# Band attention scores over all 128 partition rows: one head's queries with zeros beside them, against the keys of both heads

## The chip, the cores and the metric

The kernel runs on one core of a Trainium2 chip. The metric is the device time of one execution in microseconds (us), taken as the median of several runs.

## What is computed

One inference step of two encoder layers over 544 tokens: a prompt of 512 and a sample of 32 that also has cached keys and values. Each layer is a SwiGLU feed-forward block, a mixer and another feed-forward block, with norms around each. The mixer of the even layer is two attentions side by side, A (latent attention, "mla") and B (band attention). Only B is touched:

```python
def band_attend(q, k, v, q_pos, k_pos, rel_table):
    b, nq, h, d = q.shape                       # 8 heads, d = 64
    rel = jnp.clip(q_pos[:, None] - k_pos[None, :], -B_MAX_REL, B_MAX_REL) + B_MAX_REL
    bias = rel_table.astype(jnp.float32)[:, rel]
    s = jnp.einsum('bqhd,bkhd->bhqk', q, k).astype(jnp.float32) * HEAD_SCALE + bias[None]
    p = attn_probs(s, (k_pos >= 0)[None, :])
    return jnp.einsum('bhqk,bkhd->bqhd', p.astype(v.dtype), v).reshape(b, nq, h * d)
```

The prompt's queries see their own chunk of 64 and the eight before it, which for 512 tokens is every earlier chunk. The 32 sample queries see 256 cached keys and their own 32.

## The kernel before

Everything lies transposed in SBUF: channels on the 128 partitions, tokens along the free axis. Weights come from HBM through `w_raw`; ScalarE writes their high part `w_hi` (L351) and VectorE the low part `w_lo` (L358), and TensorE forms each product of the large projections from three matmuls (L417 to L419). Six sub-layers run one after the other: ffn, even, ffn, ffn, odd, ffn.

In the even sub-layer, `qkvb` `[128, 12, 544]` holds the queries (tiles 0 to 3), keys (4 to 7) and values (8 to 11) of the band attention. A tile of 128 rows holds two heads: the even head in rows 0 to 63, the odd one in rows 64 to 127. Then come, in TensorE's order: the latent attention (`attention("mla")`), a short preparation (`band_ready`, L753 to L785), the band attention (`attention("band")`), and the output projection.

Each attention works through items. The first 32 are the prompt's: 8 heads, each with 4 blocks of 128 queries against 128, 256, 384 and 512 keys. The last two are the sample's, four heads each, every head in 32 output rows of its own. For each item TensorE forms the scores in one of three PSUM banks (L570 for band, L564 for mla, L580 for the odd layer's "swa"), adds masks or the relative bias by a matmul with the identity (L549: `rel_hi` and `rel_lo` for band, one mask of 128 columns for mla), VectorE takes the row maximum (L1255), ScalarE the exponentials (L889), TensorE turns the probabilities (L615), ScalarE copies them back (L900), TensorE multiplies them with the values (L639, for the sample L653), and VectorE scales the result (L1279, L1282). The loop of TensorE runs the scores of item n, then the turn of item n - 3 and the values of item n - 4, so that other work of TensorE lies between an item's scores and its turn. After every second head, four blocks of outputs are turned (L666). Scores of the sample are L586 and L549 (bias), then for each head L597 (its own 32 keys) and L600 (256 cached keys, `kB_cache`).

The scores of one band head use only its own 64 rows of both operands. Those of mla use 96 rows (64 channels and 32 rotary ones).

`band_ready` turns the values of `qkvb` into `vB` (L765), forms the bias tiles (L768, L772, L775), and waits for ScalarE and VectorE to have copied them out (L1124, L1427, L1430) and for two DMAs, which GpSimd issues once the last mla scores are done (L1507 to L1509). GpSimd then waits for the fourth sub-layer (L1511). `qtA` and `ktA`, the operands of the mla scores, lie from `kt_at` up to `kt_at + 43008`; nothing reads them after the last mla scores.

Of the kernel before, what the change touches and what calls it, by code (L numbers as in the profile page):

```python
# [25 lines left out]
F32 = mybir.dt.float32  # L26
# [5 lines left out]
P = 128  # L32
D = 1024
KD = D // P
SEQ, DEC, PAST = 512, 32, 256
T = SEQ + DEC
# [9 lines left out]
NOPE, ROPE, HD = 64, 32, 64  # L46
# [5 lines left out]
SK = DEC + PAST  # L52
# [83 lines left out]
def build(nc, ins, outs):  # L136
    with ExitStack() as ctx:
        cursor = [(nc.sbuf_base + 31) // 32 * 32]

        def place(name, shape, dt, at=None):  # L140

            size = 4 * int(np.prod(shape[1:]))
            offset = cursor[0] if at is None else at
            if at is None:
                cursor[0] += (size + 31) // 32 * 32
            return nc.alloc_sbuf_tensor_at(name, shape, dt, offset=offset)
# [37 lines left out]
        qkvb = place("qkvb", [P, 12, T], F32, at=arena)  # L184
        kt_at = arena + 26112
# [21 lines left out]
        kB_cache = place("kB_cache", [P, 4, PAST], F32, at=kt_at + 14336)  # L207
        rel_hi = place("rel_hi", [P, NH, 2 * P], F32R, at=kt_at + 18432)
        relS_hi = place("relS_hi", [P, 2, SK], F32R, at=kt_at + 26624)
        rel_lo = place("rel_lo", [P, NH, 2 * P], F32R, at=va_at)  # L210
        relS_lo = place("relS_lo", [P, 2, SK], F32R, at=va_at + 8192)

# [26 lines left out]
        psum = ctx.enter_context(nc.psum_tensor("psum", [P, 8, 512], F32))  # L239

        def sem(name):
            return ctx.enter_context(nc.semaphore(name))
# [41 lines left out]
        kpe_spread = sem("kpe_spread")  # L284
        band_in = sem("band_in")
        band_prep = sem("band_prep")
        rel_in = sem("rel_in")
        rel_shifted = sem("rel_shifted")
        mask_in = sem("mask_in")
# [132 lines left out]
        def _(pe):  # L422
# [93 lines left out]
            def out_projection(s):  # L516
# [7 lines left out]
                for m, H in out_order(SUBS[s]):  # L524
# [10 lines left out]
                    out_half(s, g + m // 2, (g + m // 2) % 2, m % 2, H, m == 0, mid)  # L535
                    before = (m, H)

            def attention(name, between=None):

                items, done = ATT[name]  # L540
# [10 lines left out]
                def scores(n):  # L551

                    it, bank = items[n], n % 3
                    if name == "swa" and n in (8, 16):

                        pe.wait_ge(c_roped, n + 2)
                    if n >= 3:

                        pe.wait_ge(exp_done, base + n - 2)
                    if it["kind"] == "prompt":  # L560
                        i, w = it["i"], it["width"]
                        q = slice(P * i, P * (i + 1))
                        if name == "mla":
                            nc.tensor.matmul(psum[:, bank, 0:w], qtA[:, it["h"], q], ktA[:, it["h"], 0:w],  # L564
                                             start=True, stop=True)
                            mm = add(psum[:, bank, w - P:w], maskE[:, P:2 * P])
                        elif name == "band":
                            h, near = it["h"], min(w, 2 * P)
                            r = slice(64 * (h % 2), 64 * (h % 2) + 64)
                            nc.tensor.matmul(psum[:, bank, 0:w], qkvb[r, h // 2, q], qkvb[r, 4 + h // 2, 0:w],  # L570
                                             start=True, stop=True)

                            add(psum[:, bank, w - near:w], rel_hi[:, h, 2 * P - near:2 * P])
                            mm = add(psum[:, bank, w - near:w], rel_lo[:, h, 2 * P - near:2 * P])
                        else:
                            lo = P * max(i - 1, 0)
                            for d in range(2):
                                h = it["h"] + 2 * d
                                r = slice(64 * (h % 2), 64 * (h % 2) + 64)
                                nc.tensor.matmul(psum[:, bank, d * w:(d + 1) * w], qtC[r, h // 2, q],  # L580
                                                 kdup[r, h // 8, lo:lo + w], start=True, stop=True)
                                mm = add(psum[:, bank, d * w:(d + 1) * w], maskC[:, 2 * P - w:2 * P])
                    else:
                        if name == "band":

                            nc.tensor.matmul(psum[:, bank, 0:SK], unit[:], relS_hi[:, it["h"] // 4, :],  # L586
                                             start=True, stop=True)
                            add(psum[:, bank, 0:SK], relS_lo[:, it["h"] // 4, :])
                        for d in range(4):
                            h = it["h"] + d  # L590
                            rows = slice(32 * d, 32 * d + 32)
                            r = slice(64 * (h % 2), 64 * (h % 2) + 64)
                            if name == "mla":
                                mm = nc.tensor.matmul(psum[rows, bank, 0:SK], qtA[:, h, SEQ:T],
                                                      ktA[:, h, SEQ:KEYS_A], start=True, stop=True)
                            elif name == "band":
                                nc.tensor.matmul(psum[rows, bank, 0:DEC], qkvb[r, h // 2, SEQ:T],  # L597
                                                 qkvb[r, 4 + h // 2, SEQ:T], start=False, stop=True,
                                                 skip_group_check=True)
                                mm = nc.tensor.matmul(psum[rows, bank, DEC:SK], qkvb[r, h // 2, SEQ:T],  # L600
                                                      kB_cache[r, h // 2, :], start=False, stop=True,
                                                      skip_group_check=True)
                            else:
                                mm = nc.tensor.matmul(psum[rows, bank, 0:DEC + P], qtC[r, h // 2, SEQ:T],
                                                      kdup[r, h // 8, SEQ:KEYS_C], start=True, stop=True)
                    mm.then_inc(s_ready, 1)
# [146 lines left out]
            def band_ready(s):  # L753

                def job(j):
                    if j == 5:
                        pe.wait_ge(rel_shifted, 10)
                        pe.wait_ge(o_lo, O0["band"])
                    if j >= 8:

                        pe.wait_ge(band_act if j % 2 == 0 else band_dve, (j - 8) // 2 + 1)
                    if j < 5:
                        n = P if j < 4 else DEC
                        for v in range(4):
                            mm = nc.tensor.transpose(psum[0:n, j, v * P:(v + 1) * P],  # L765
                                                     qkvb[:, 8 + v, j * P:j * P + n], ident[:])
                    elif j < 9:
                        nc.tensor.matmul(psum[:, j % 8, :], flips[:, 0, :],  # L768
                                         hankel[:, 2 * (j - 5):2 * (j - 4), :].rearrange("p h k -> p (h k)"),
                                         start=True, stop=True)  # L770
                        for h in range(2):
                            mm = nc.tensor.matmul(psum[:, j % 8, 2 * P * h:2 * P * (h + 1)], identE[:], maskE[:],  # L772
                                                  start=False, stop=True, skip_group_check=True)
                    else:
                        mm = nc.tensor.matmul(psum[:, j % 8, 0:SK], flips[:, 1, :], hankelS[:, j - 9, :],  # L775
                                              start=True, stop=True)
                    mm.then_inc(band_prep, 1)

                pe.wait_ge(exp_done, A0["band"])
                pe.wait_ge(pt_ready, A0["band"])  # L780
                for j in range(11):
                    job(j)
                pe.wait_ge(band_act, 9)
                pe.wait_ge(band_dve, 8)
                pe.wait_ge(band_in, 16 * 2)  # L785

            pe.wait_ge(consts_in, 16 * 3)
            for s, kind in enumerate(SUBS):
# [9 lines left out]
                elif kind == "even":  # L798
                    for f in range(2, 8):
# [3 lines left out]
                        if f == 4:  # L803

                            pe.wait_ge(proj_read, P0[s] + 4)
                            for H in range(2):
                                pe.wait_ge(lat_sq, 3 * H + 3)
                                for t in range(2):
                                    nc.tensor.matmul(psum[:, 4 + H, 0:TH], ones[:], scratch[:, 2 * H + t, :],
                                                     start=t == 0, stop=t == 1)  # L810
                                nc.tensor.matmul(psum[:, 6 + H, 0:TH], ones[:], lat_rstd[:, 1, HALF[H]],
                                                 start=True, stop=True).then_inc(lat_stat, 1)
# [655 lines left out]
        def _(pool):  # L1468
# [4 lines left out]
            rows = slice(NOPE, QK)  # L1473
# [33 lines left out]
            pool.wait_ge(s_ready, A0["band"])  # L1507
            load(vB_cache[:], ins["band_v_cache"]).then_inc(band_in, 16)
            load(kB_cache[:], ins["band_k_cache"]).then_inc(band_in, 16)  # L1509
            s = 4  # L1510
            pool.wait_ge(y_ready, 16 * s)  # L1511
            load(ropeC[:], ins["rope_swa"]).then_inc(odd_in, 16)
# [127 lines left out]
```

## Time and profile before

| | |
|---|---|
| median of 3 runs | 2331.65 us (2329.54 to 2334.93) |
| span of the profiled execution (first to last instruction) | 2321.0 us |
| what lies around that span, against the median | 10.65 us |
| TensorE busy | 2276.4 us, 98% |
| TensorE weight loads busy | 2172.6 us, 94% |
| VectorE busy | 1033.6 us, 45% |
| ScalarE busy | 777.3 us, 33% |
| GpSimd busy | 20.4 us, 1% |
| mean granted clock of TensorE | 0.973 of 2.4 GHz |
| HBM | 75 GB/s over the span |

The profile gives no time for the profiled execution other than its span, so a time for a kernel is read here as span plus 10.65 us. Busy time of TensorE is modelled at the ends of its instructions: a record lasts longer than its turn in the pipeline, so the cost of a matmul is read from the distance between the starts of two records. An fp32 matmul shows as two records. A granted clock of 1.00 is 2.4 GHz, and 0.50 is 1.2 GHz.

### The profile page before, as it was taken

How to read it: one execution, taken by the hardware profiler on the slowest of the kernel's cores; microseconds unless marked ns; L12 is line 12 of the kernel's file. 1: busy time of each engine (PE TensorE's matmuls, PEld its weight loads, DVE VectorE, ACT ScalarE, POOL GpSimd, SP SyncE). 2: the span in 40 equal slices, each digit the busy share in tenths (PEclk: the TensorE clock that was granted, in tenths of full speed). 3: DMA queues.
4: the chain of work that ended last, by engine and by line, in shares of the span. 5: the costliest groups of instructions: out<-in, count | busy, mean ns of one | idle time of the engine just before them, and what ended most of it. 6: DMA issues, size and time to landing. Idle time of an engine off the chain costs nothing.

```text
span 2321.0 us, 41718 instructions
## 1 busy us (share of the span) xinstructions
PE 2276.4 (98%) x16934; PEld 2172.6 (94%) x16934; DVE 1033.6 (45%) x1992; ACT 777.3 (33%) x1566; POOL 20.4 (1%) x42
## 2 busy tenths in 40 slices
PE   7999999999999999999999999999999999999997
PEld 6999999998767999999999999999987799999997
DVE  4544412656532274444126544512666555444313
ACT  4332322423532353333124323322425453332211
POOL 0000000001000000000000000000000000000000
PEclk9999999999955999999999999999999999999999
DMA  3222322124000122222221222322220022222221
GB/s 114 92 90 90 104 76 93 59 82 144 19 1 1 55 67 97 88 81 98 76 93 55 91 90 90 96 83 93 71 85 1 19 73 86 79 89 90 99 76 63
DMA packets 48489, 176.94 MB, mean 76 GB/s; under 512 B 5808, under 2 KB 10240, under 8 KB 48144
## 3 DMA queue, kind: packets, MB, share of 16 engines
q1 hardware_dynamic: 46144, 166.66, 22.0%
q0 software_dynamic: 2256, 9.03, 1.2%
q8 instruction: 63, 1.03, 0.2%
q14 instruction: 26, 0.21, 0.0%
HBM read 168.93 MB, written 5.36 MB: 75 GB/s over the span
## 4 chain that ended last, share of the span: by engine, by line
PE 94%; DVE 3%; ACT 2%; issue 0%; DMA 0%; SPq 0%; DVEq 0%; ACTq 0%
PE psum L418 26%; PE psum L417 26%; PE psum L419 26%; PE psum L639 3%; PE psum L494 2%; PE psum L549 2%; PE psum L570 2%; PE psum L446 2%; PE psum L615 2%; PE psum L580 2%; PE psum L564 1%; PE psum L653 1%; DVE w_lo L358 1%; ACT xhi L964 0%; DVE rstd L1165 0%; DVE y_ffn L1173 0%
## 5 line engine op out<-in xcount | busy, mean ns | idle before, releaser
L417 PE MATMUL psum<-xhi,w_hi 128*128 128x272 f32 x3488 | 1031.7, 296 | 19.5 <-DVE w_lo L358 16.8
L418 PE MATMUL psum<-xlo,w_hi 128*128 128x272 f32 x3488 | 1005.5, 288 | 0.0
L419 PE MATMUL psum<-xhi,w_lo 128*128 128x272 f32 x3488 | 1003.4, 288 | 0.0
L417 PEld LDWEIGHTS psum<-xhi,w_hi 128*128 128x128 f32 x3488 | 657.9, 189 | 25.0 <-issue 16.8
L418 PEld LDWEIGHTS psum<-xlo,w_hi 128*128 128x128 f32 x3488 | 657.5, 188 | 5.3
L419 PEld LDWEIGHTS psum<-xhi,w_lo 128*128 128x128 f32 x3488 | 656.3, 188 | 0.0
L358 DVE TENSOR_TENSOR w_lo<-w_raw,w_hi 128x1024 fp32r<-128x1024 f32 (+1 forms) x286 | 363.0, 1308 | 444.3 <-ACT w_hi L351 443.9
L417 PE MATMUL psum<-h_hi,w_hi 128*128 128x272 f32 x1408 | 417.2, 296 | 0.0
L418 PE MATMUL psum<-h_lo,w_hi 128*128 128x272 f32 x1408 | 405.7, 288 | 0.0
L419 PE MATMUL psum<-h_hi,w_lo 128*128 128x272 f32 x1408 | 403.9, 287 | 0.0
L351 ACT ACTIVATE w_hi<-w_raw 128x1024 fp32r<-128x1024 f32 (+1 forms) x286 | 307.4, 1120 | 80.5 <-PE psum L419 70.2
L417 PEld LDWEIGHTS psum<-h_hi,w_hi 128*128 128x128 f32 x1408 | 265.1, 188 | 2.4
L418 PEld LDWEIGHTS psum<-h_lo,w_hi 128*128 128x128 f32 x1408 | 264.9, 188 | 2.4
L419 PEld LDWEIGHTS psum<-h_hi,w_lo 128*128 128x128 f32 x1408 | 264.4, 188 | 0.0
L1007 ACT ACTIVATE scratch<-scratch 128x272 f32<-128x272 f32 x160 | 69.0, 431 | 551.3 <-DVE scratch L1222 551.3
L1222 DVE TENSOR_TENSOR scratch<-psum,rstd 128x272 f32<-128x272 f32 x176 | 77.7, 441 | 313.1 <-PE psum L419 311.4
L1022 ACT ACTIVATE y_ffn<-psum 128x272 f32<-128x272 f32 (+1 forms) x64 | 25.3, 396 | 379.6 <-PE psum L419 379.6
L1231 DVE TENSOR_TENSOR h_lo<-scratch,h_hi 128x272 f32 (+1 forms) x176 | 77.8, 442 | 119.3 <-ACT h_hi L1009 111.4
L1255 DVE TENSOR_REDUCE soft<-psum 128x1 f32<-128x128 f32 (+5 forms) x104 | 54.3, 523 | 118.0 <-PE psum L549 113.4
L1165 DVE RECIPROCAL rstd<-rstd 128x272 f32<-128x272 f32 x24 | 44.4, 1851 | 140.0 <-ACT rstd L947 106.9
L1009 ACT ACTIVATE h_hi<-scratch 128x272 f32 (+1 forms) x160 | 69.1, 432 | 95.7 <-DVE scratch L1228 95.7
L1228 DVE TENSOR_TENSOR scratch<-scratch 128x272 f32<-128x272 f32 x176 | 77.8, 442 | 26.7 <-ACT scratch L1007 8.2
(219 smaller groups left out, 1696.4 us busy)
## 6 DMA issues: line engine op xcount, KB each, us to landing
w_raw<-in_w_gate_up SPq DMA_DIRECT2D x176, 512.0 KB, 4.0
w_raw<-in_w_down SPq DMA_DIRECT2D x64, 704.0 KB, 5.0
w_raw<-in_even_in SPq DMA_DIRECT2D x16, 512.0 KB, 3.5
w_raw<-in_odd_in SPq DMA_DIRECT2D x10, 512.0 KB, 3.7
w_raw<-in_even_out SPq DMA_DIRECT2D x8, 512.0 KB, 4.1
w_raw<-in_odd_out SPq DMA_DIRECT2D x8, 512.0 KB, 3.8
x<-in_x SPq DMA_DIRECT2D x2, 1088.0 KB, 7.5
out_band_kv<-qkvb POOLq DMA_DIRECT2D x1, 2176.0 KB, 9.0
```

Source lines behind the costliest of these rows:

```text
L351: nc.scalar.activation(w_hi[:, 2 * par + u, 0:n], w_raw[:, u, 0:n], ACT.Copy).then_inc(w_hi_done, 1)
L358: nc.vector.tensor_tensor(w_lo[:, 2 * par + u, 0:n], w_raw[:, u, 0:n], w_hi[:, 2 * par + u, 0:n].bitcast(F32), ALU.subtract).then_inc(w_lo ...
L417: nc.tensor.matmul(out, s_hi, m_hi, start=first, stop=False)
L418: nc.tensor.matmul(out, s_hi, m_lo, start=False, stop=False)
L419: return nc.tensor.matmul(out, s_lo, m_hi, start=False, stop=last)
L639: mm = nc.tensor.matmul(psum[:, bank, HD * d:HD * (d + 1)], probsT[:, n % 2, p:p + P], v, start=j == 0, stop=j == per - 1)
L1007: nc.scalar.activation(scratch[:, 2 * H, :], scratch[:, 2 * H, :], ACT.Silu).then_inc(silu_done, 1)
L1009: nc.scalar.activation(h_hi[:, f, HALF[H]], scratch[:, 2 * H, :], ACT.Copy).then_inc(hhi_ready, 1)
L1222: nc.vector.tensor_tensor(scratch[:, 2 * H, :], psum[:, bank, 0:TH], rstd[:, HALF[H]], ALU.mult).then_inc(gate_scaled, 1)
L1228: nc.vector.tensor_tensor(scratch[:, 2 * H, :], scratch[:, 2 * H, :], scratch[:, 2 * H + 1, :], ALU.mult).then_inc(h_ready, 1)
L1231: nc.vector.tensor_tensor(h_lo[:, f, HALF[H]], scratch[:, 2 * H, :], h_hi[:, f, HALF[H]].bitcast(F32), ALU.subtract).then_inc(hlo_ready, 1)
L1255: red = nc.vector.tensor_reduce(part[:, 0:heads], scores, AX_X, ALU.max, negate=True)
```

## The change

A new tile `qB_odd` `[128, 4, 544]` takes the odd heads' queries: GpSimd copies them into its rows 64 to 127, sets its rows 0 to 63 to zero, and then sets rows 64 to 127 of the query tiles of `qkvb` to zero. So `qkvb` holds each even head's queries with zeros beside them, and `qB_odd` each odd head's. The score matmuls take all 128 rows of both operands; the other head's keys meet zeros. `qB_odd` lies at `kt_at + 31232`, within what was `qtA`. The rest of the kernel stays as it was.

```diff
+        qB_odd = place("qB_odd", [P, 4, T], F32, at=kt_at + 31232)
...
+            def q_alone(h):
+
+                return qB_odd if h % 2 else qkvb
...
                             h, near = it["h"], min(w, 2 * P)
-                            r = slice(64 * (h % 2), 64 * (h % 2) + 64)
-                            nc.tensor.matmul(psum[:, bank, 0:w], qkvb[r, h // 2, q], qkvb[r, 4 + h // 2, 0:w],
+                            nc.tensor.matmul(psum[:, bank, 0:w], q_alone(h)[:, h // 2, q], qkvb[:, 4 + h // 2, 0:w],
                                              start=True, stop=True)
...
-                                nc.tensor.matmul(psum[rows, bank, 0:DEC], qkvb[r, h // 2, SEQ:T],
-                                                 qkvb[r, 4 + h // 2, SEQ:T], start=False, stop=True,
+                                nc.tensor.matmul(psum[rows, bank, 0:DEC], q_alone(h)[:, h // 2, SEQ:T],
+                                                 qkvb[:, 4 + h // 2, SEQ:T], start=False, stop=True,
                                                  skip_group_check=True)
-                                mm = nc.tensor.matmul(psum[rows, bank, DEC:SK], qkvb[r, h // 2, SEQ:T],
-                                                      kB_cache[r, h // 2, :], start=False, stop=True,
+                                mm = nc.tensor.matmul(psum[rows, bank, DEC:SK], q_alone(h)[:, h // 2, SEQ:T],
+                                                      kB_cache[:, h // 2, :], start=False, stop=True,
                                                       skip_group_check=True)
...
                 pe.wait_ge(band_act, 9)
                 pe.wait_ge(band_dve, 8)
+                pe.wait_ge(q_parted, 3)
                 pe.wait_ge(band_in, 16 * 2)
...
             load(vB_cache[:], ins["band_v_cache"]).then_inc(band_in, 16)
             load(kB_cache[:], ins["band_k_cache"]).then_inc(band_in, 16)
+            nc.gpsimd.tensor_copy(qB_odd[HD:P, :, :], qkvb[HD:P, 0:4, :]).then_inc(q_parted, 1)
+            nc.gpsimd.memset(qB_odd[0:HD, :, :], 0.0).then_inc(q_parted, 1)
+            pool.wait_ge(q_parted, 1)
+            nc.gpsimd.memset(qkvb[HD:P, 0:4, :], 0.0).then_inc(q_parted, 1)
             s = 4
```

## Rows read from the trace of the kernel before

**Rows 1.** The page: TensorE's clock in 40 slices, and the chain by engine.

```profile
PEclk9999999999955999999999999999999999999999
...
PE 94%; DVE 3%; ACT 2%; issue 0%; DMA 0%; SPq 0%; DVEq 0%; ACTq 0%
```

**Rows 2.** Windows: mla, band, swa items (span, PE, PEld, DVE, ACT, POOL, PEclk, DMA).

```profile
576.60:622.70 46.10, 45.26 (x319) 38.05 (x319) 25.90 (x87) 30.11 (x94) 0.00 (x0) 1.00 0.01 1
...
646.20:754.70 108.50, 108.46 (x352) 77.14 (x352) 27.33 (x89) 31.45 (x96) 0.00 (x0) 0.51 0.00 1
...
1724.90:1819.50 94.60, 94.24 (x529) 68.24 (x528) 63.24 (x236) 49.88 (x190) 0.00 (x0) 1.00 0.00 1
```

**Rows 3.** Timeline, TensorE: band items of 128 and 512 keys (start us, us).

```profile
739.77 0.79 PE L570 MATMUL psum<-qkvb 64*128 64x128 f32 x2
...
740.98 0.65 PE L615 MATMUL psum<-ident,probsE 128*128 128x128 f32 x2
...
750.32 2.07 PE L570 MATMUL psum<-qkvb 64*128 64x512 f32 x2
...
752.91 0.41 PE L615 MATMUL psum<-ident,probsE 128*128 128x128 f32 x1
```

**Rows 4.** Timeline, TensorE: mla items of 512 and 128 keys, at full clock.

```profile
583.60 1.08 PE L564 MATMUL psum<-ktA,qtA 96*128 96x512 f32 x2
...
584.58 0.27 PE L615 MATMUL psum<-ident,probsE 128*128 128x128 f32 x1
...
585.52 0.44 PE L564 MATMUL psum<-ktA,qtA 96*128 96x128 f32 x2
...
585.86 0.41 PE L615 MATMUL psum<-ident,probsE 128*128 128x128 f32 x2
```

**Rows 5.** Timeline, TensorE: swa scores of 128 and 256 keys, 64 rows, full clock.

```profile
1725.58 0.48 PE L580 MATMUL psum<-kdup,qtC 64*128 64x128 f32 x2
...
1726.25 0.70 PE L580 MATMUL psum<-kdup,qtC 64*128 64x256 f32 x2
...
1727.19 0.70 PE L580 MATMUL psum<-kdup,qtC 64*128 64x256 f32 x2
```

**Rows 6.** Windows, TensorE: where its clock moves (span, PE busy, PEclk, DMA).

```profile
633.40:634.90 1.50, 0.02 (x1) 1.00 0.00 0
...
635.00:635.50 0.50, 0.50 (x4) 0.58 0.00 0
...
638.50:639.00 0.50, 0.50 (x6) 1.00 0.00 0
...
648.50:649.00 0.50, 0.50 (x3) 0.73 0.00 0
...
757.50:758.00 0.50, 0.50 (x3) 0.54 0.00 0
```

**Rows 7.** Timeline: the second bias add at full clock, near the start of band.

```profile
647.62 0.39 PE L549 MATMUL psum<-rel_hi,identE 128*128 128x256 f32 x1
647.85 0.28 PE L549 MATMUL psum<-rel_lo,identE 128*128 128x256 f32 x1
```

**Rows 8.** Timeline: the start of the first and of the second sample item of band.

```profile
754.68 0.59 PE L586 MATMUL psum<-relS_hi,identE 128*128 128x288 f32 x1
...
757.34 0.59 PE L586 MATMUL psum<-relS_hi,identE 128*128 128x288 f32 x1
```

**Rows 9.** Timeline: GpSimd's last DMA issue, and what the first band scores wait for.

```profile
625.71 0.55 POOL L1509 DMA_DIRECT2D kB_cache<-in_band_k_cache  x1
...
646.24 0.46 PE L570 MATMUL psum<-qkvb 64*128 64x128 f32 x2 [1.22 <-ACT relS_hi L1124]
```

**Rows 10.** Groups by line: GpSimd's memsets, and VectorE's slowest elementwise rows (busy us, mean ns).

```profile
L1479 POOL MEMSET ckv_hi<- 128x96 f32 x1 | 0.2, 217 | 0.0
...
L1627 POOL MEMSET const-float32-0.0<- 128x1 f32 x1 | 0.1, 93 | 0.3 <-issue 0.3
...
L1165 DVE RECIPROCAL rstd<-rstd 128x272 f32<-128x272 f32 x24 | 44.4, 1851 | 140.0 <-ACT rstd L947 106.9 <-ACT rstd L953 33.2
```

More of the change, by code:

```diff
@@ L286, in build @@
         band_prep = sem("band_prep")
+        q_parted = sem("q_parted")
         rel_in = sem("rel_in")
```

## Prediction

> **What bounds the kernel now.** I read the page first. The chain that ended last is TensorE for 94% of the span, so a change is worth what it takes from TensorE's own time or from a wait of TensorE. The slices of the clock show one place, slices 12 and 13, where the granted clock is 5 tenths instead of 9 or more [rows 1]. One slice is 58 us, so something like 110 us run at 1.2 GHz. The windows by stage put it in the band attention: its 32 prompt items fill 646.2 to 754.7 us with TensorE busy for 108.46 of 108.50 us and a mean clock of 0.51, while the mla attention, which has the same number of items with the same numbers of keys, takes 46.1 us at 1.00 [rows 2]. VectorE is busy for 27.3 us and ScalarE for 31.5 us of the band stretch [rows 2], so neither is the bound there; what sets the pace is TensorE.
>
> I then took the stage apart by the timeline. From the start of an item's scores to the turn that follows them, a band item takes 1.21 us for 128 keys (739.77 to 740.98) and 2.59 us for 512 (750.32 to 752.91) [rows 3]. The same distance for mla is 0.34 us (585.52 to 585.86) and 0.98 us (583.60 to 584.58) [rows 4]. In mla each further 128 keys cost (0.98 - 0.34) / 3 = 0.213 us, which is 4 x 128 columns at 2.4 GHz: an fp32 score goes over its columns four times, an added mask once. What is left of 0.34 after 0.213 for the scores and 0.053 for the mask is 0.07 us that doesn't depend on width. For the swa scores, which use 64 rows at full clock, the distance from one score to the next is 0.67 us for 128 keys and 0.94 us for 256 [rows 5]; the step of 0.27 us is again four passes and one added mask, but 0.67 - 0.267 leaves 0.40 us fixed. So scores of 64 rows cost 0.40 - 0.07 = 0.33 us an item beside others of 128 rows, at full clock, whatever their width. For band at 1.2 GHz, 1.21 us less 0.427 (scores) and 0.213 (two bias adds) leaves 0.57 us, and 2.59 less 1.707 and 0.427 leaves 0.46 us.
>
> The Trainium skill, TensorEngine Tiling (Array Packing), Key Properties, says that changing the tiling mode, not just the tile, drains TensorE. The trace agrees, with that 0.33 us.
>
> Last I looked where the clock moves [rows 6]. It falls within 635.0 to 635.5 us, after the mla sample values and a stretch in which TensorE was busy for 0.02 of 1.50 us, and is back at 638.5, while TensorE turned the values of band (L765), all over 128 rows. It falls again within 648.5 to 649.0, after a wait of 1.22 us ahead of the first band scores [rows 9] and two and a half items of 64-row scores, and then stays at 1.2 GHz until 757.5 to 758.0 without an idle moment, that is until the last 64-row score of 512 keys is 5 us past. Scores of 64 rows alone don't pull it down: the swa stage runs 94.6 us at 1.00 with them [rows 2]. But after a fall, no stretch made up largely of them brought it back, and a stretch of full-row work did.
>
> **The change part by part.** (1) *The 32 prompt items.* The new items are mla items with more bias. To mla's 46.1 us [rows 2] comes first a bias add of 256 columns instead of 128 in 24 of 32 items: 24 x 128 / 2.4 GHz = 1.3 us. Then a second bias add in all 32: at least its columns, 256 / 2.4 GHz = 0.107 us, at most the 0.23 us from `rel_hi` to `rel_lo` [rows 7]. mla's fixed 0.07 us for a score and an add makes 0.035 us each, so I take 0.107 + 0.035 = 0.14 us, times 32 = 4.5 us (3.4 to 7.4). Together 51.9 us (50.8 to 54.8) for what took 108.4 us (646.24 [rows 9] to 754.68 [rows 8]): **56.5 us** less. Some 10.6 us of this, 32 x 0.33, are the switches between 64 and 128 rows, and 46 us the clock. VectorE's 27.3 and ScalarE's 31.5 us stay below 51.9, and mla ran with 25.9 and 30.1 in 46.1 us [rows 2], so they should not become the bound.
>
> (2) *The sample items.* The first one, 754.68 to 757.34, ran at 1.2 GHz [rows 8], as did the first 0.6 us of the second. At full clock 2.66 us become 1.33 and 0.6 become 0.3: **1.6 us** less (1.0 to 1.7, since some of it is not streaming). That their scores take 128 rows by 32 instead of 64 by 32 I cost at nothing: four heads lie in four column groups either way. All that follows, the sample values and the output projection, was at full clock and stays.
>
> (3) *GpSimd's copy and two memsets*, each of 64 rows x 2176 columns. GpSimd's DMA issue ends at 625.71 + 0.55 = 626.3 us, and the scores could start at 646.24 [rows 9], so 19.9 us cover them. A memset takes (217 - 93) / 95 = 1.3 ns a column [rows 10]: 2.9 us each, 5.8 for two. A GpSimd copy is not in the trace. From below it costs the memset's 2.9 us; from above I take VectorE's slowest elementwise row, 1851 ns for 272 columns or 6.8 ns a column [rows 10], which makes 14.8 us. I take 4 us, near the memset, since a copy has the same output and one input. Sum 9.8 us, done at about 636 us (8.7 to 20.6 us, 635.0 to 646.9). So the cost is **nothing**, 0.7 us at the upper end. Without the cover the wait on `q_parted` would hold every band score, and with it all that follows on TensorE. Behind the three instructions GpSimd has nothing to do before the fourth sub-layer, and no DMA issue of it or of SP is moved past them. VectorE works on the bias rows in the same stretch; should its 2.2 us of `hankel` shifts (L1416), which lie on the chain, take twice as long beside GpSimd, that would be 2.2 us. I take 0 and keep 2.2 for the range.
>
> (4) *The clock's fall at 648.5.* The 1.22 us wait ahead of the first score stays, since it is for the last bias rows of ScalarE and VectorE [rows 9]. If the clock falls there all the same and comes back as at 638.5, after 3.4 us, it costs half of that, 1.7 us. The sample values may bring such a fall in one place more or fewer than before. I take 0 for both and keep -1.7 and +3.4.
>
> Sum: 56.5 + 1.6 = 58.1 us off. The span goes from 2321.0 to 2262.9 us and, with the 10.65 us around it, the median from 2331.65 to **2273.5 us**. The bounds: at best 57.6 + 1.7 + 1.7 = 61 us off, at worst 53.6 + 1.0 - 0.7 - 2.2 - 3.4 = 48.3. The median itself moves by up to 3 us among the runs shown. The forecast's own range is 2268 to 2284.
>
> **The rivals.** *The clock stays at 1.2 GHz.* Half of each score's rows are zeros, and what the clock follows may not be the rows that an instruction names. For it: TensorE was already busy throughout at 0.51 [rows 2], so it isn't plain that another form of the same scores wakes it. Against it: the fall is gone after full-row work at 638.5, and mla with 96 rows never lost the clock. Then only the switches go, 32 x 0.33 = 10.6 us, or 32 x (0.46 - 0.14) = 10.2 to 32 x (0.57 - 0.14) = 13.8 from the items at 1.2 GHz: **2321 us** (2317 to 2322).
>
> The Trainium skill, TensorE: Matmul & The Clock Gate, Part 1, says that the clock follows how busy TensorE has been of late and that sustained work releases it. By that rule the band stretch should have been at full speed already, and more rows would change nothing in it: the rival's time. The trace doesn't agree, with 0.51 at 108.46 of 108.50 us busy; I leave the rival its chance for that.
>
> *The clock comes back only for parts of the stage.* The turns and the values of 64 columns lie between the scores, and falls and returns could alternate. For it: two falls within 14 us before [rows 6]. Against it: mla holds 1.00 through the same alternation. With the stage at half clock for half of its work it takes 1.5 x 51.9 = 78 us, and the time is **2300 us**, anything from 2285 to 2315.
>
> *GpSimd is late, and the kernel slower.* Place: the wait on `q_parted` at the end of `band_ready`. GpSimd needs more than 19.9 us before it costs anything and 19.9 + 58.1 = 78 us before it decides: 12 ns a column over 3 x 2176 columns. At 14 ns a column it takes 91 us, and the time is 2273.5 + 71.5 = **2345 us**. Against it: its memset row has 1.3 ns a column, and the slowest elementwise row of any engine 6.8 [rows 10].
>
> **How the numbers follow.** Forecast 0.82, clock stays low 0.08, partly low 0.06, GpSimd late 0.02, and 0.02 for a stage whose time doesn't move for reasons that I don't see. A difference under 0.2%, 4.7 us, is about what a measurement of this kernel can't tell from none. The first three are faster by more than that, save for a little of the second: faster 0.95, same 0.03, slower 0.02. For 8 in 10, the range takes the forecast's own, 2 us more below, and the edge of the partly low case: 2266 to 2287.
>
> **What would show it.** In the profile after, slices 12 and 13 should have no 5. From the first L570 to the first L586 it should be 50 to 55 us at a mean clock of 0.97 or more; a band item from score to turn about 0.45 us for 128 keys and 1.15 for 512. GpSimd's three instructions should end by about 636 us and not release L570. The prediction is wrong if the clock stays at 0.5 in spite of full rows (the stage then near 98 us), if the first L570 waits for GpSimd, or if the waits of TensorE for L889 or L1282 grow once it runs twice as fast.

## The result and the profile after

The changed kernel takes 2265.68 us (median of 4 runs, 2263.59 to 2268.53) against 2330.61 for the kernel before: a ratio of 0.9725, with a 95% interval of 0.971 to 0.9739. That is 64.9 us less. The forecast was 2273.5 us, in a range of 2266 to 2287, so the time lies 7.8 us under the point and 0.3 us under the lower end of the range, which is less than the spread of its own runs. In the profiled executions the span went from 2321.0 to 2266.7 us, 54.3 us less; why this is 10.6 us short of the difference of the medians is taken up below.

The page of the kernel after shows the clock by slices without the two fives, and TensorE's share of the chain as it was:

```profile
span 2266.7 us, 41722 instructions
...
PEclk9999999999999999999999999999999999999999
...
PE 94%; DVE 3%; ACT 2%; issue 0%; DMA 0%; SPq 0%; DVEq 0%; ACTq 0%
```

Windows of the kernel after, by stage: the mla items, the band items, the band sample items with their values, the swa items. The columns are those of [rows 2].

```profile
576.60:622.70 46.10, 44.44 (x313) 37.08 (x311) 26.32 (x87) 29.38 (x93) 0.00 (x0) 1.00 0.01 1
649.10:699.20 50.10, 49.80 (x351) 42.92 (x351) 25.89 (x87) 30.23 (x94) 0.00 (x0) 1.00 0.01 1
699.20:710.00 10.80, 10.80 (x123) 7.93 (x122) 4.50 (x19) 4.17 (x13) 0.00 (x0) 1.00 0.01 2
1668.10:1762.70 94.60, 94.23 (x529) 68.22 (x528) 63.24 (x236) 49.97 (x190) 0.00 (x0) 1.00 0.00 1
```

The 32 band items take 50.1 us at 1.00 where they took 108.5 at 0.51, with as many matmul records (351 and 352; some are missing from any profile) and about the same work on VectorE and ScalarE (25.9 and 30.2 us busy, 27.3 and 31.5 before). The swa stage, which nobody touched, takes its 94.6 us again.

Timeline of TensorE in the kernel after, an item of 512 keys and one of 128; L575 is what was L570, and L620 what was L615:

```profile
656.82 1.08 PE L575 MATMUL psum<-qkvb,qB_odd 128*128 128x512 f32 x2
657.34 0.68 PE L555 MATMUL psum<-rel_hi,identE 128*128 128x256 f32 x1
657.86 0.28 PE L555 MATMUL psum<-rel_lo,identE 128*128 128x256 f32 x1
657.98 0.27 PE L620 MATMUL psum<-ident,probsE 128*128 128x128 f32 x1
...
658.93 0.44 PE L575 MATMUL psum<-qkvb 128*128 128x128 f32 x2
...
659.38 0.41 PE L620 MATMUL psum<-ident,probsE 128*128 128x128 f32 x2
```

From score to turn an item now takes 1.16 us (657.98 - 656.82) instead of 2.59 and 0.45 us instead of 1.21 [rows 3]. The second bias add costs 0.12 us, its columns and almost nothing else (657.98 - 657.86).

Timeline of the kernel after, GpSimd and what the first scores wait for:

```profile
627.01 0.55 POOL L1515 DMA_DIRECT2D kB_cache<-in_band_k_cache  x1
...
627.61 2.00 POOL L1516 COPY qB_odd<-qkvb 64x2176 f32<-64x2176 f32 x1
...
629.66 1.90 POOL L1517 MEMSET qB_odd<- 64x2176 f32 x1
...
631.62 1.91 POOL L1519 MEMSET qkvb<- 64x2176 f32 x1
...
637.85 2.19 DVE L1422 TENSOR_SCALAR hankel<-hankel,rel_far 128x256 f32<-128x256 f32 x8
...
649.14 0.46 PE L575 MATMUL psum<-qkvb 128*128 128x128 f32 x2 [1.22 <-ACT relS_hi L1130]
```

GpSimd's three instructions, which part the queries, end at 633.5 us. The first score waits as before, for the bias rows and for the same 1.22 us [rows 9].

Windows of TensorE in the kernel after, where its clock is low (columns as in [rows 6]):

```profile
641.50:644.00 2.50, 2.50 (x6) 0.50 0.00 0
...
1774.50:1784.50 10.00, 10.00 (x53) 0.50 0.01 2
```

Two low stretches of the kernel before have moved: the one at 635 us begins at 641 and now lies on the bias matmuls, and one follows the swa stage, with its sample values and the start of the output projection, for 10 us instead of 3.4. A third, of 3.4 us, stands at 518 us, where before had none.

The stretch at 1774.5 us is a second place where TensorE is busy without a break (10.00 of 10.00 us above, and its last idle moment 3.6 us earlier was 0.28 us long) and yet loses the clock. Most of it are the values of the sample, 64 columns each, on 128 rows by 32 columns of the array and on 32 by 32 in turn:

```profile
1770.86 0.27 PE L658 MATMUL psum<-vC_cache,probsTC 128*32 128x64 f32 x2 [0.28 <-DVE osbC L1288]
...
1778.54 0.42 PE L658 MATMUL psum<-vC_cache,probsTC 128*32 128x64 f32 x2
1778.89 0.42 PE L658 MATMUL psum<-vC,probsTC 32*32 32x64 f32 x2
```

### The profile page after: what moved, and what is told of

Same layout as the page of the kernel before. It is cut to its first block, busy times and chain, and to the rows that moved or that the text cites. A ratio compares the mean times of both kernels' runs of the same rounds, so it can differ in the third digit from the quotient of the medians.

```text
span 2266.7 us, 41722 instructions
## 1 busy us (share of the span) xinstructions
PE 2220.2 (98%) x16934; PEld 2139.1 (94%) x16934; DVE 1033.2 (46%) x1992; ACT 777.1 (34%) x1566; POOL 26.3 (1%) x45
## 4 chain that ended last, share of the span: by engine, by line
PE 94%; DVE 3%; ACT 2%; issue 0%; DMA 0%; SPq 0%; DVEq 0%; ACTq 0%
PE psum L420 27%; PE psum L419 26%; PE psum L421 26%; PE psum L644 2%; PE psum L496 2%; PE psum L448 2%; PE psum L585 2%; PE psum L620 1%; PE psum L555 1%; PE psum L575 1%; PE psum L658 1%; PE psum L570 1%; DVE w_lo L360 1%; ACT xhi L970 0%; DVE rstd L1171 0%; DVE y_ffn L1179 0%
## 5 line engine op out<-in xcount | busy, mean ns | idle before, releaser
L1261 DVE TENSOR_REDUCE soft<-psum 128x1 f32<-128x128 f32 (+5 forms) x104 | 54.2, 522 | 60.1 <-PE psum L555 58.2
```

What stands on the lines that cost most here:

```text
L1261: red = nc.vector.tensor_reduce(part[:, 0:heads], scores, AX_X, ALU.max, negate=True)
```

## The experiments

All medians are of four or more runs unless said otherwise. The ratios are to the kernel before, measured beside each run: 2327.04 us for again, warm64, nozero and half, 2331.74 for late and swa_full, 2329.56 for pause and late3, 2330.61 for the changed kernel itself. So a difference between medians of two lines of this list is uncertain by some microseconds. Here "stage" is the time from the first band score to the first sample item, which the change takes from 108.4 to 50.1 us.

**again.** The kernel before, unchanged.

> The kernel before, unchanged, profiled once more, because its first profile has a span of 2321.0 us while its runs have a median of 2330.6. My reading: the prompt part of the band stage lasts 108.4 us at half clock in every execution, and what differs is short falls of the clock elsewhere, some 8 us in all against the first profile. The rival is that the band stage itself was shorter in the profiled execution than in most: then the first L570 to the first L586 would take about 116 us here. Time 2330 (2326 to 2335).

2327.72 us against 2327.04 for before, a ratio of 1.0005 (0.9988 to 1.0023). Windows of its band stage:

```profile
646.50:754.60 108.10, 108.10 (x351) 76.84 (x351) 27.36 (x89) 31.46 (x96) 0.00 (x0) 0.51 0.00 1
```

The stage is as long as in the first profile, but this profile too fell on a short execution, with a span of 2319.8 us. Time less span is about 1.8 us in every run (2.0 to 2.2 in late), so the 10.65 us of the front table are not a fixed surrounding: about 8 of them are a difference between executions. Half of the other 22 runs have a span near 2325.1 us and a mean clock of 0.971, seven more a span near 2327.8; the profiled one has 0.974 and 2319.8. Lost to the low clock are 2325.1 x 0.029 = 67.4 and 2319.8 x 0.026 = 60.3 us: 7 us, which covers the difference of 5.3 (a last digit of the clock is 2.3 us of span). So the longer executions have more low clock, but no profile shows where. One run of 22 took 2310.96 us at a clock of 0.979. It is 10.6 us shorter than the profiled one, which has only 3.4 us of low clock ahead of the stage and some 8 at the very end (half of them, 6 us, is all that they can give back), so the long fall itself was probably shorter in that run; no profile shows this either.

**warm64.** The kernel before with the pause ahead of the scores filled:

```diff
                 for j in range(11):
                     job(j)
+                pe.wait_ge(band_dve, 2)
+                for _i in range(2):
+                    nc.tensor.matmul(psum[:, 3, :], flips[:, 0, :],
+                                     hankel[:, 0:2, :].rearrange("p h k -> p (h k)"), start=True, stop=True)
```

> The kernel before with two more matmuls of 128 rows x 512 columns, written to a bank that nobody reads, in the pause of 1.22 us ahead of the first band scores; the scores stay at 64 rows. Theory A (64-row scores keep a clock that they find, as in the swa stage, and only can't bring it back): no fall at the start, the stage takes the 50.1 us of the changed kernel plus 32 x 0.33 = 10.6, about 61 us, and the time is 2330.6 - 47 = 2283 us. Theory B (a stage of 64-row scores falls whatever goes before it): the stage stays near 108 us, at 0.50, and the time is 2331 us, the same as before within 2 us.

2282.46 us, a ratio of 0.9796 (0.9774 to 0.9818). Timeline and then windows of its band stage:

```profile
647.75 1.88 PE L785 MATMUL psum<-hankel,flips 128*128 128x512 f32 x4
649.56 0.48 PE L570 MATMUL psum<-qkvb 64*128 64x128 f32 x2
```

```profile
649.60:709.70 60.10, 60.10 (x352) 43.44 (x352) 26.56 (x87) 30.63 (x94) 0.00 (x0) 1.00 0.00 1
```

Theory A holds, to within a microsecond. With 64-row scores all through, the stage ran at 1.00 once the pause ahead of it was gone, and the times of all four runs say the same. With the pause and full-row scores behind it, in the changed kernel, it ran at 1.00 too. So the fall at 648.5 [rows 6] took both, the pause and the 64-row scores. This run also parts the gain in two: 108.4 - 60.1 = 48.3 us are the clock, and 60.1 - 50.1 = 10.0 us what 64-row scores cost at the same clock, 0.31 us an item, which is put down here to the switching between 64 and 128 rows.

**nozero.** The changed kernel without GpSimd's part, both heads' queries in the same rows:

```diff
             def q_alone(h):
-                return qB_odd if h % 2 else qkvb
+                return qkvb
...
-                pe.wait_ge(q_parted, 3)
...
-            nc.gpsimd.tensor_copy(qB_odd[HD:P, :, :], qkvb[HD:P, 0:4, :]).then_inc(q_parted, 1)
-            nc.gpsimd.memset(qB_odd[0:HD, :, :], 0.0).then_inc(q_parted, 1)
-            pool.wait_ge(q_parted, 1)
-            nc.gpsimd.memset(qkvb[HD:P, 0:4, :], 0.0).then_inc(q_parted, 1)
```

> The changed kernel without the parting: GpSimd copies and clears nothing, and the scores of both heads of a pair take all 128 rows of the same queries, so each score is the sum of two heads' scores. This tells whether zeros in half of the rows matter to the clock or to the time. If only the rows that the instruction names count: 2266 us, as the changed kernel, the stage 50 us at 1.00. If zeros weigh less: some stretches of the changed kernel that ran at 0.5 (about 3.4 us at 640 us) are gone and the time is 2 to 4 us lower. If GpSimd's 5.8 us of work cost anything, that goes too: up to 2 us.

2265.89 us (2265.79 to 2266.08), a ratio of 0.9728 (0.9712 to 0.9744), against 2265.68 for the changed kernel; its stage lasts from 646.6 to 696.7 us:

```profile
646.60:696.70 50.10, 49.84 (x352) 42.93 (x352) 25.99 (x87) 30.25 (x94) 0.00 (x0) 1.00 0.01 1
```

Neither the zeros nor GpSimd's work show in the time, and the clock of the stage is 1.00 with zeros in half of the rows and without.

**half.** The changed kernel with the odd heads' scores back on 64 rows:

```diff
-                            nc.tensor.matmul(psum[:, bank, 0:w], q_alone(h)[:, h // 2, q], qkvb[:, 4 + h // 2, 0:w],
+                            r = slice(HD, P) if h % 2 else slice(0, P)
+                            nc.tensor.matmul(psum[:, bank, 0:w], q_alone(h)[r, h // 2, q], qkvb[r, 4 + h // 2, 0:w],
```

> The changed kernel, but the odd heads' scores take 64 rows again (from rows 64 to 127 of the new tile); the even heads keep 128. Theory A (a clock that is up stays up with 64-row scores among full-row work; each item of 64 rows costs 0.33 us of switching): stage at 1.00, 50.1 + 16 x 0.33 = 55.4 us, time 2265.7 + 5.3 = 2271 us. Theory B (a stretch of mostly 64-row scores of 384 and 512 keys pulls the clock down): falls in the odd heads and returns in the even ones, mean clock near 0.75, stage 75 to 85 us, time 2290 to 2300 us.

2275.56 us, a ratio of 0.9771 (0.9754 to 0.9787). Windows of its stage:

```profile
649.00:703.80 54.80, 54.77 (x351) 43.12 (x351) 26.53 (x87) 30.50 (x94) 0.00 (x0) 1.00 0.00 1
```

The stage came out as theory A has it, 4.7 us over the changed kernel's, or 0.29 us for each of 16 items. The median is 9.9 us over, though. Between the two profiled executions, of 2272.7 and 2266.7 us, the difference is 6.0 us, and that is accounted for: 4.7 us in the stage, and 1.7 because the low stretch after the swa stage lasts 13.7 us instead of 10.2. The rest of the 9.9 us lies in executions that were not profiled. Differences of a few microseconds between these kernels are therefore read from the stage, not from the median.

**late.** GpSimd busy for ten memsets more before its copy:

```diff
-                pe.wait_ge(q_parted, 3)
+                pe.wait_ge(q_parted, 13)
...
+            for _i in range(10):
+                nc.gpsimd.memset(qB_odd[0:HD, :, :], 0.0).then_inc(q_parted, 1)
+                pool.wait_ge(q_parted, _i + 1)
             nc.gpsimd.tensor_copy(qB_odd[HD:P, :, :], qkvb[HD:P, 0:4, :]).then_inc(q_parted, 1)
```

> The changed kernel with ten more memsets of 64 x 2176 on GpSimd ahead of its copy (1.9 us each, one after the other), so that the parting ends at about 653 us instead of 633.5 and the first score waits for it: about 4 to 5 us later than 649.1, after a pause of TensorE of 5 to 6 us instead of 1.2. Two questions in one: where the cover of GpSimd ends (15.6 us after the copy and the two memsets), and whether full-row scores bring back a clock that has fallen. Theory (full rows bring it back): the clock falls in the pause, the band stage begins at 0.5 and is at 1.00 after 3 to 7 us, costing 2 to 3 us, so the time is 2265.7 + 4.5 + 2.5 = 2272 to 2274 us. Rival (full rows only keep a clock that they find): the stage stays at 0.5, near 98 us, and the time is 2265.7 + 4.5 + 48 = 2318 us.

2285.7 us, a ratio of 0.9806 (0.979 to 0.9822), 20 more than the changed kernel, where 6 to 8 were expected, and not by the way that was expected. Its timeline, VectorE, GpSimd and TensorE:

```profile
640.05 15.62 DVE L1422 TENSOR_SCALAR hankel<-hankel,rel_far 128x256 f32<-128x256 f32 x8
...
653.58 1.94 POOL L1522 MEMSET qkvb<- 64x2176 f32 x1
655.60 0.63 DVE L1425 TENSOR_SCALAR hankelS<-hankelS,far 128x288 f32<-128x288 f32 x2
...
656.28 2.07 PE L773 MATMUL psum<-hankel,flips 128*128 128x512 f32 x2 [15.30 <-DVE hankelS L1425]
...
665.20 0.46 PE L575 MATMUL psum<-qkvb 128*128 128x128 f32 x2 [1.22 <-ACT relS_hi L1130]
```

GpSimd was done at 655.5 (653.58 + 1.94), and the first score came at 665.2 and waited for the bias rows, not for GpSimd. What was late was VectorE: its eight `hankel` shifts took 15.62 us instead of 2.19, each about as long as one of GpSimd's instructions beside it, and were over when GpSimd was. The two matmul groups of the bias (L773, L777) and all behind them followed. Between the profiled executions the difference is 16.0 us; the first score is 16.1 us later, of which the shifts are 13.4 and 2.2 were there before they began. The fallen clock was up again during the bias matmuls, so full-row work brought it back, but the scores never met a fallen clock; in the next run they do.

**pause.** ScalarE holds the first score back instead:

```diff
                         nc.scalar.activation(out, src, ACT.Copy).then_inc(band_act, 1)
+                    for i in range(3):
+                        nc.scalar.activation(hankel[:].rearrange("p h k -> p (h k)"),
+                                             x[:].rearrange("p k t -> p (k t)")[:, 0:2048],
+                                             ACT.Copy).then_inc(band_act, 1)
+                        act.wait_ge(band_act, 10 + i)
...
-                pe.wait_ge(band_act, 9)
+                pe.wait_ge(band_act, 12)
```

> The changed kernel with three copies of 2048 columns on ScalarE after its last bias row, for which the first band score waits: TensorE pauses for about 7 us instead of 1.2, with its clock up at the beginning of the pause. GpSimd and VectorE are left alone, so this asks only what becomes of a clock that falls right ahead of full-row scores. Full rows bring it back: the clock is at 0.5 for the pause and the first 2 to 7 us of the stage, then 1.00; the stage is 51 to 54 us long, and the time is 2265.7 + 5.8 + 1 to 3 = 2273 us. Full rows only keep a clock that they find: the stage stays at 0.5 as it did with 64 rows, near 98 us, and the time is 2265.7 + 5.8 + 48 = 2320 us.

2275.27 us, a ratio of 0.977 (0.9748 to 0.9792). Windows of it, the pause, the first 3.5 us of the stage, and the rest of the stage:

```profile
647.50:653.50 6.00, 0.00 (x0) 0.00 (x0) 0.97 (x3) 5.92 (x4) 0.00 (x0) 0.75 0.00 0
653.50:657.00 3.50, 3.46 (x11) 2.79 (x11) 0.72 (x2) 0.92 (x4) 0.00 (x0) 0.50 0.02 5
657.50:705.50 48.00, 47.73 (x342) 41.15 (x340) 25.22 (x85) 29.20 (x90) 0.00 (x0) 1.00 0.00 1
```

The clock fell in the pause, the full-row scores began at 1.2 GHz, and some 4 us later it was back for good: a stage of 52.0 us, as expected of full rows that bring it back. The time is 9.6 us over the changed kernel's, where 7 to 9 were expected. The kernel before, whose clock fell 2 to 3 us behind the first score and not ahead of it, stayed at 1.2 GHz for 109 us [rows 2, 6]. So in this stage the full-row scores both kept the clock and brought it back; the 64-row scores, among the same other work, only kept it.

**late3.** As late, with three memsets instead of ten.

> The changed kernel with three more memsets on GpSimd instead of ten, so that its work ends at about 639.4 us on the first profile's clock, 1.5 us after VectorE starts the hankel shifts (L1422). With ten, one of these shifts took 2022 ns instead of 348 while GpSimd was at work. If VectorE's SBUF-to-SBUF operation waits for a running GpSimd instruction to end: one or two of the eight shifts take up to 2 us, the stage starts 1 to 2 us later, and the time is 2267 us (2266 to 2269). If it needs a longer overlap to hurt: 2265.7, the same.

2270.76 us (2265.06 to 2272.93), a ratio of 0.9757 (0.9734 to 0.9779), 4 to 5 us over what was expected of either. The groups by line of its stretch from 639 to 656 us have the shifts at 479 ns in the mean instead of 348:

```profile
L1422 DVE TENSOR_SCALAR hankel<-hankel,rel_far 128x256 f32<-128x256 f32 x8 | 3.3, 479 | 0.0
```

That is 1.1 us more, for an overlap of 1.3 us (639.09 to 640.39), and it lies on the path. The rest of the median is not this: the profiled run of the same kernel took 2265.06 us at a mean clock of 0.997, the others had 0.992 to 0.995.

**after2.** The changed kernel once more, one run.

> The changed kernel once more, for one more profile beside the others: the band stage 50.1 us at 1.00, and short falls of the clock in other stages that need not stand where the first profile had them (518, 641 and 1775 to 1785 us).

2267.05 us at a mean clock of 0.994. Its low stretches are at 634.5 (3.4 us) and 1771 us (13.7 us), and none at 518: the short ones move from one execution to the next.

**again2.** The kernel before once more, one run.

> The kernel before once more, for one more profile: how much time at half clock it has outside of the band stage. The first two profiles have a fall of 3.4 us at 635 us and the long one of 109.2 us, and spans of 2321.0 and 2319.8, while most runs have spans of 2325 to 2328 us. If what differs is one or two more short falls, a profile with such a span shows them, most likely in the swa stage; if it is the long one, its length is more than 109.2 us.

2321.6 us; again the short kind of execution, its stage 108.2 us, with low stretches only at 635.5 and 649. It doesn't answer its question.

**swa_full.** The changed kernel, and in the odd layer the keys of even and odd heads in two tiles with zeros beside them:

```diff
-                                nc.tensor.matmul(psum[:, bank, d * w:(d + 1) * w], qtC[r, h // 2, q],
-                                                 kdup[r, h // 8, lo:lo + w], start=True, stop=True)
+                                nc.tensor.matmul(psum[:, bank, d * w:(d + 1) * w], qtC[:, h // 2, q],
+                                                 k_alone(h)[:, h // 8, lo:lo + w], start=True, stop=True)
...
+            nc.gpsimd.memset(kdup[HD:P, :, :], 0.0).then_inc(k_zero, 1)
+            nc.gpsimd.memset(kodd[0:HD, :, :], 0.0).then_inc(k_zero, 1)
...
-                    pool.dma_start(kdup[64 * r:64 * r + 64, kv, 0:T], kC[64 * kv:64 * kv + 64, :]).then_inc(k_doubled, 16)
+                    pool.dma_start((kodd if r else kdup)[64 * r:64 * r + 64, kv, 0:T], kC[64 * kv:64 * kv + 64, :]).then_inc(k_doubled, 16)
```

> The changed kernel with the same thing done in the odd layer's swa attention, where the keys are copied twice anyway: the even heads' keys go into rows 0 to 63 of one tile whose other rows are zero, the odd heads' into rows 64 to 127 of a second one, and the scores take all 128 rows of queries and keys. No work is moved to GpSimd but two memsets of 64 x 1344 columns, 1.2 us each. If each 64-row score beside full-row work costs 0.33 us: 64 prompt scores make 21 us, less what VectorE (63.2 us busy in a stage of 94.6) begins to bound, so 15 to 21 us, and the short falls of the clock in and after this stage (5 us lost in the changed kernel) may go too: 2265.7 - 18 = 2248 us (2242 to 2252). Rival: the stage is bound by the chain of waits between VectorE, ScalarE and TensorE, and loses under 5 us: 2261 us or more.

2250.68 us (2248.61 to 2252.57), a ratio to the kernel before of 0.9655 (0.9639 to 0.9671), 15 us under the changed kernel: the fastest of all. Windows of its swa stage, and a place in its timeline where TensorE now waits:

```profile
1665.00:1742.50 77.50, 73.88 (x529) 67.68 (x528) 61.65 (x234) 49.02 (x189) 0.00 (x0) 1.00 0.00 1
```

```profile
1670.26 0.73 PE L837 MATMUL psum<-qtC,swapC 128*128 128x272 f32 x2 [1.08 <-DVE qtC L1255]
```

The stage went from 94.6 to 77.5 us with the clock at 1.00 in both, so the clock has no part in this. The 17.1 us come near to what the switching predicts: 64 scores x 0.31 = 19.8 us, less the idle time that appears (77.5 - 73.9 = 3.6 us), for VectorE's rotations of the queries (L1255) above all. Its low stretch after the stage is still there, 13.7 us long.

## Why the prediction was right, point by point

**What bounds the stage**, right. TensorE's records fill the stage before and after, and VectorE and ScalarE stay at 25.9 and 30.2 of 50.1 us. That 64-row scores cost something fixed beside full-row work, 0.33 us an item by [rows 4, 5], is shown: 0.31 by warm64, 0.29 by half.

**The 32 prompt items**, right in kind, 1.8 us off in size: 51.9 us were forecast and 50.1 came. One term at fault is the second bias add, taken at 0.14 us an item (4.5 us in all) and found at 0.12 (0.107 are its columns), which makes 0.6 us; the other 1.2 us are not traced to a row. The parts, 46 us for the clock and 10.6 for the switches, were 48.3 and 10.0.

**The sample items**, right: from the first sample item to the last output turn 12.0 us became 10.6, so 1.4 us for the forecast 1.6.

**GpSimd hidden**, right, and by more than was thought: 2.00 us for the copy (4 forecast), 1.9 for each memset (2.9), done at 633.5 us. But the reason for its cover was wrong. The prediction measured the cover to the first score, 19.9 us, and allowed 2.2 us for VectorE beside GpSimd. The runs show that the cover ends where VectorE's `hankel` shifts begin, 4.3 us after the third instruction (637.85 - 633.5). Ten memsets more cost 13.4 us there, not 2.2. So that GpSimd's work cost nothing was owed to 4.3 us of distance that the prediction never looked at, and the rival of a late GpSimd was put at the wrong wait.

**The fall at 648.5 us**, right that it costs nothing: with full-row scores behind the same 1.22 us pause the clock stays up. What the prediction said of the stage, that the clock falls at a pause with 64-row scores behind it and that these scores don't bring it back, is shown by warm64 on the one side and pause on the other. Why they don't is open. A 64-row score differs from a full one in two things at once, the rows that it names and the switch of some 0.3 us to and from the 128-row work beside it, and a busy record may hide such a switch; no run parts the two. The low stretch at 1774.5 us in the sample values, half of which name all 128 rows but switch their form every time, would fit either.

**The time**, 7.8 us under the point, and just under the range. Of the 7.8 us, 1.6 are that stage and samples gave 59.7 us instead of 58.1, 1.0 that the median of before is 2330.61 with a fourth run and not 2331.65, and 5.2 are the rest of the 64.9, which lies outside of stage and samples. The clocks of the runs speak for short stretches of low clock, which lie differently in every execution. The profiled pair shows them with the other sign: 1.3 us lost ahead of the last mla item to the stretch at 518, 1.6 in the preparation, where a stretch of the same length now lies on the bias matmuls, 2.5 behind the band stage. Together they make 54.3 of 59.7. So the step that was weak is the conversion from span to median, "span plus 10.65 us": 1.8 us lie around a span, and the rest was the distance between a short execution and the median. That the medians differ by 5.2 us more than the stage is measured; where the kernel before has the additional low clock stays open, since three profiles of it all fell on short executions. One place is likely: eight of the nine profiles of the other kernels have a low stretch of 10.2 to 13.7 us after the swa stage, the three of before 3.4 us or none. If its longer executions have it as well, half of it, 5.1 to 6.8 us, is an estimate of what is lost there, near the 5.3 to 8.0 us that they are longer. The profiled execution of the changed kernel, for its part, is the longest of its four runs, and lies 1.0 us above their median, not 10.65 below. That the two profiled executions would differ as the medians do was assumed, and was 10.6 us off.

**The rivals.** The clock staying low is excluded: the zeros are no hindrance (nozero), and a fallen clock was back some 4 us after the first full-row score (pause). Partly low did not happen in the stage in any profile of the changed kernel. GpSimd late and slower is far off, but late shows that its point of decision was nearer than 78 us.

The Trainium skill, TensorE: Matmul & The Clock Gate, Part 1, has the clock follow how busy TensorE has been. Here it stayed at 0.51 for 108 us of a TensorE that was busy without a break [rows 2], and was at 1.00 for the same work once the scores named 128 rows, or once it had not fallen. Busy time as the profile's records count it doesn't foretell the clock in this kernel.

## What to carry to other kernels

Look at the granted clock by slices before anything else: here half clock in a stage that was busy throughout cost 48 us, and the wait ahead of it that set it off only 1.22. Where a stage of 64-row matmuls among full-row work sits at 1.2 GHz, this kernel had two ways out, and they can be had apart: fill the pause at which the clock fell (two wasted matmuls took 48.3 us off the stage and 44.6 us off the median), or name all 128 rows, with zeros in one operand, which also takes away the switching, some 0.3 us for each 64-row matmul among full-row ones, at full clock too. Where the second operand is copied anyway, put the zeros there; it then costs two memsets.

## What the runs showed of the hardware that was not expected

In the run late VectorE's operations from SBUF to SBUF stood still for as long as GpSimd worked: eight `tensor_scalar` of 256 fp32 columns took 15.62 us beside GpSimd's memsets and 2.19 without, while VectorE's operations that read PSUM kept their time (L1288, 281 ns in the mean beside the memsets, 284 in the changed kernel after GpSimd was done). The Trainium skill, SBUF — State Buffer, Who interferes with whom, says that VectorE's two-port modes and GpSimd lock each other out of a shared pair of ports for a whole instruction; the trace agrees as to the length of the wait, with 2022 ns in the mean for a shift against 348, and 1.9 us for a memset. In which mode the shifts ran it doesn't show.

A score product of 128 rows, half of them zeros, took no longer than mla's of 96 rows, and less than the same product on 64 rows at the same clock: from score to turn 1.16 us against 1.40 for 512 keys and 0.45 against 0.69 for 128. The rest of the 0.31 us of an item falls outside of this distance. The figures for 64 rows are from the timeline of warm64:

```profile
693.89 0.49 PE L570 MATMUL psum<-qkvb 64*128 64x128 f32 x2
...
694.58 0.41 PE L615 MATMUL psum<-ident,probsE 128*128 128x128 f32 x2
...
699.19 1.12 PE L570 MATMUL psum<-qkvb 64*128 64x512 f32 x2
...
700.59 0.27 PE L615 MATMUL psum<-ident,probsE 128*128 128x128 f32 x1
```
